# The second mixer's input units in another order, seven of them split into halves instead of fp32

## Chip, cores and metric

The kernel runs on one core of one Trainium2 chip. The metric is device time in microseconds, the median of several runs. Lower is better.

## What is computed

The reference runs two transformer blocks one after the other on x of 256 tokens by 2048 features, in float32. The part that changes is the start of the second block:

```
h = rms_norm(x, mix_norm_g)
proj = h @ w_in                      # 2048 x 4656
q, kv, gate_logits, conv_in = split(proj)
attn = nsa_attention(q, kv, sigmoid(gate_logits), rel_bias, cmp_pos, cmp_w1, cmp_w2)
conv = conformer_conv(conv_in, ...)  # a * sigmoid(gate), causal conv of 31 taps, layer norm, silu
x = x + concatenate([attn, conv]) @ w_out
```

`kv` holds keys and values for three branches: one is compressed by a small MLP over blocks of 32 tokens (`compress`), two are used as they are (the branches 0 and 1 below). `conv_in` is 1024 channels of `a` and 1024 of gate.

## The kernel before

The whole network is one list of units, made by `all_units` (line 138). A unit is 256 output columns of one weight matrix. Its weights come in subs of 512 KB: 4 k-tiles of 128 rows for 256 columns, so an input unit with 16 k-tiles has 4 subs. Activations lie feature-major, 128 features by 256 tokens per tile.

A unit has a mode. In mode `full` the weights go to TensorE as fp32 straight from the landing buffer RAW, against H in fp32. H must first be multiplied in place by the norm weights (`full_u2`, line 1202, on ScalarE, four phases of four tiles). In mode `one` each sub is split: ScalarE writes a rounded high half WH, VectorE writes WL = RAW - WH (`split`, lines 1169 and 1695), and TensorE multiplies three times with 256 columns: high with high, high with low, low with high. Modes `nat`, `turn` and `joint` are forms of the split one. There are 4 RAW buffers and 5 of each half.

The second mixer's input units are, with the names used in this text: a0 to a3 (`ev_ca`, the channels a), g0 to g3 (`ev_cg`, the gate), m0 and m1 (`ev_cmp`, keys and values to compress), k0 and k1 (`ev_k2`), v0 and v1 (`ev_v2`), q0 to q3 (`ev_q2`, queries of four heads each). Before, they run in this order, `full` except a0, g0, v0, v1: a0 g0 m0 m1 a1 g1 k0 k1 a2 g2 v0 v1 q0 a3 g3 q1 q2 q3. Then come the eight units of w_out on the convolution's rows (`ev_add`) and the eight on the attention's.

`make_plan` (line 265) turns the units into one order of steps that every engine follows, each taking those it has a part in. Each engine works its own list strictly in order. After each sub the plan takes one phase from a lane `conv` and one from a lane `side`. When a unit's last sub is in the plan, its evacuation (`evac`) follows (for a0 and pg7 two subs later), and the work it makes possible is appended to a lane: `conv31` of 11 phases (62 instructions of VectorE, 60 of them multiply-adds of 256 columns, six in each phase but the first), `compress` of 3, `dup_k2` of 2, `attn2` of 9, `ln` of 7, `scc` of 1. `before=("side",)` empties the side lane ahead of a unit, `2` makes it two stages wide. `split` of a sub stands 4 subs ahead of it when the sub four places before it in its buffer is split too, else 2 (`lead`, line 294). The fetch of a sub is on SP's queue and waits until its RAW buffer is free: for a split sub after `split`, for a fp32 one after its products. SP's queue also carries the loads of W1K and W1V (`load_w1`, line 656, 1 MB each, weights of `compress`) and of BM (`load_bias`, line 659, 2 MB, the attention's bias). Sub numbers here: a0 562 to 565, g0 566 to 569, then four per unit (v1 six, 606 to 611), q0 612, q3 632 to 635.

A unit's columns go to the next PSUM bank of 0, 1, 2, from q0 on of 0, 1, and TensorE waits until the unit that had the bank is evacuated (`bank_free`, line 766). BLK, GTM and GCM are buffers of `compress`, KTC holds m's or k's columns, TA and TC the gate's and a's, SCC (in SQA) the convolution's sums for the layer norm, SX2, PT2 and RC the attention's, CC the convolution's outputs.

Of the kernel before, what the change touches and what calls it, by code (L numbers as in the profile page):

```python
# [27 lines left out]
HOLD = 2  # L28
LATE = 3
FULL_XBC = 7  # L30

MATS = ["rot", "rdup0", "rdup1", "triu", "negT", "dup0", "dup1", "ident", "ones"]

VECS = [("g_mix", 16), ("cw", 96), ("cb", 24), ("g_ssd", 16), ("dsk", 16), ("g_ffn", 16), ("g_ple", 16),
# [72 lines left out]
def stage(name, i, n, late=0, gaps=()):  # L107

    out = [None] * late
    for ph in range(n):  # L110
        out.append(ph)
        if ph in gaps:
            out.append(None)
    return (name, i, out)
# [15 lines left out]
def attn1_stage(t, late):  # L130
    return stage("attn1", t, 4, late, (1, 2))


def attn2_stage(t, late):
    return stage("attn2", t, 9, late)


def all_units():
    us = []
    add = lambda *p, **k: us.append(Unit(*p, **k))  # L140
    order = lambda i: "turn" if i else "joint"
    wide = (0, 1, 2, 3)
    for i in range(4):
        add("w_in", 0, 16, 256 * i, "U1", "ev_q", i, mode=order(i), mid=(("norm", 0, 0),) if i == 0 else (), hold=2 if i == 0 else 0,
            gens=([stage("rotary", 0, 3)] if i == 0 else []) + [stage("rope_q", i, 2)])
    add("w_in", 0, 16, 1024, "U1", "ev_k", 0, mode="turn", gens2=[stage("full_u1", 0, 4)], gens=[stage("rope_k", 0, 2), stage("rope_k", 1, 2)])
    add("w_in", 0, 16, 1280, "U1", "ev_v", 0, nc=288, more=6656, nat=True, mode="nat",
        gens=[2] + [attn1_stage(t, LATE if t == 1 else 0) for t in range(8)] + [1, stage("cums", 0, 2)])
    for i in range(12):
        add("w_in", 0, 16, 3584 + 256 * i, "U1", "ev_xbc", i, mode="full" if i < FULL_XBC else "turn",  # L150
            gens2=[stage("conv4", i, 3)] + ([stage("dt", 0, 2)] if i == 0 else []))
    for i in range(8):
        add("w_in", 0, 16, 6688 + 256 * i, "U1", "ev_ga", i, mode="turn", before=("all",) if i == 0 else (),
            gens=[stage("ssd", g, 6) for g in range(4)] if i == 0 else (), pace=2)
        add("w_attn_br", 0, 8, 256 * i, "AT", "ev_oa", i, mode="turn", pace=2)
    for i in range(8):
        add("w_in", 0, 16, 1536 + 256 * i, "U1", "ev_z", i, mode="turn", banks=wide,
            before=("side",) if i == 0 else ())
    for i in range(8):
        add("w_in", 0, 16, 8736 + 256 * i, "U1", "ev_gs", i, mode="turn", banks=wide, mid=(("norm", 1, 0),) if i == 0 else (),  # L160
            hold=HOLD if i == 0 else 0)
    for i in range(8):
        add("w_ssd_br", 0, 16, 256 * i, "YH", "ev_os", i, mode=order(i), banks=wide)
    for i in range(8):
        add("w_o", 0, 16, 256 * i, "MH", "ev_h", i, mode=order(i), banks=wide)
    for half in range(2):
        for i in range(11):
            first = half == 0 and i == 0
            add("w_gate", 0, 16, 256 * (11 * half + i), "F1", "ev_g1", 11 * half + i, banks=wide, mode=order(11 * half + i),
                mid=(("norm", 2, 0),) if first else (), hold=HOLD if first else 0)  # L170
            add("w_up", 0, 16, 256 * (11 * half + i), "F1", "ev_u1", 11 * half + i, banks=wide, mode="turn")
        for i in range(8):
            if half and i == 3:
                us[-2].mid = (("load_p", 0, 0),)
                for j in range(8):
                    add("w_ple_proj", 0, 2, 256 * j, "PH", "ev_pp", j, banks=wide)
            add("w_down", 2816 * half, 22, 256 * i, "G1", "ev_h", 8 + 8 * half + i, banks=wide, k0=22 * half,
                mode=order(i))
    for i in range(8):
        add("w_ple_gate", 0, 16, 256 * i, "P1H", "ev_pg", i, mode=order(i), mid=(("norm", 3, 0),) if i == 0 else (),  # L180
            hold=HOLD if i == 0 else 0, banks=wide)

    def ca_cg(i, mode="full", mid=(), **k):
        add("w_in_2", 0, 16, 2608 + 256 * i, "U2", "ev_ca", i, mode=mode, mid=mid[:1] if i else mid, **k)
        add("w_in_2", 0, 16, 3632 + 256 * i, "U2", "ev_cg", i, mode=mode, banks=k.get("banks", (0, 1, 2)),
            mid=(("load_w1", 0, 0),) if i == 0 else (), gens=[stage("full_u2", 0, 4)] if i == 0 else [],
            gens2=[stage("conv31", i, 11)] + ([stage("ln", 0, 7)] if i == 3 else []))

    def k2(br):
        add("w_in_2", 0, 16, 1536 + 512 * br, "U2", "ev_k2", br, mode="full", before=("side",),  # L190
            gens=[stage("dup_k2", br, 2)])

    def q2(i, **k):
        add("w_in_2", 0, 16, 256 * i, "U2", "ev_q2", i, mode="full", gens2=[stage("scc", 0, 1), stage("scc", 1, 1)] if i == 0 else [],
            gens=[attn2_stage(2 * i, 0), attn2_stage(2 * i + 1, 2 if i == 0 else 0)], banks=(0, 1), **k)

    ca_cg(0, "one", (("load_pos", 0, 0), ("join", 0, 0)), hold=HOLD)
    add("w_in_2", 0, 16, 1024, "U2", "ev_cmp", 0, mode="full", mid=(("load_w1", 1, 0),),
        gens=[stage("compress", 0, 3, 1)])
    add("w_in_2", 0, 16, 1280, "U2", "ev_cmp", 1, mode="full", mid=(("load_bias", 0, 0),),  # L200
        gens=[stage("compress", 1, 3, 1)])
    ca_cg(1)
    k2(0)
    k2(1)
    ca_cg(2)
    add("w_in_2", 0, 16, 1792, "U2", "ev_v2", 0, nat=True)
    add("w_in_2", 0, 16, 1792 + 512, "U2", "ev_v2", 1, nc=304, nat=True, mode="nat")
    q2(0, before=("side", 2))
    ca_cg(3, banks=(0, 1))
    q2(1)  # L210
    q2(2)
    q2(3)
    for i in range(8):
        add("w_out_2", 1024, 8, 256 * i, "MXC", "ev_add", i, banks=(0, 1), before=("conv",) if i == 0 else ())
    for i in range(8):
        add("w_out_2", 0, 8, 256 * i, "MXA", "ev_h", 24 + i, mode="turn", banks=wide, before=("side",) if i == 0 else ())
    for half in range(2):
        for i in range(11):
            first = half == 0 and i == 0
            add("w_up_2", 0, 16, FFN + 256 * (11 * half + i), "F2", "ev_g2", 11 * half + i, banks=wide, mode=order(11 * half + i),  # L220
                mid=(("norm", 5, 0),) if first else (), hold=HOLD if first else 0)
            add("w_up_2", 0, 16, 256 * (11 * half + i), "F2", "ev_u2", 11 * half + i, banks=wide, mode="turn")
        for i in range(8):
            add("w_down_2", 2816 * half, 22, 256 * i, "G2", "ev_h" if not half else "ev_fin",
                32 + i if not half else i, banks=wide, k0=22 * half, mode=order(i))
    return us
# [116 lines left out]
def hybrid_block_kernel(nc, a, out):  # L343
# [104 lines left out]
    def mat(n):  # L448
        i = MATS.index(n)
        return M7[:, i, :] if i < 7 else M2[:, i - 7, :]  # L450
# [141 lines left out]
    jn_pe, jn_d, jn_a = steps("join_pe"), steps("join_d", "rr", "ms", "eps", "rec", "ru"), steps("join_root")  # L592
# [1090 lines left out]
    def vector_program(e):  # L1683
# [453 lines left out]
        def ev_cmp(n, u):  # L2137
            kv = u.i
            if kv:
                e.wait_ge(cmp_d.sem, cmp_d.at(0, "b11"))  # L2140
            else:
                e.wait_ge(blank.sem, 2)
            e.wait_ge(sub_done.sem, u.end)
            tt(KTC[:, :, :], bank(u.bank), two(RU[:, 0:T]), MUL).then_inc(cmp_d.sem)
            if kv:
                e.wait_ge(cp_pe.sem, cp_pe.at(0, "w1"))
            else:
                e.wait_ge(pos_k_in, 16)
                e.wait_ge(pos_v_in, 16)
            e.wait_ge(cmp_d.sem, cmp_d.at(kv, "k"))  # L2150
            for lh in range(2):
                for hp in range(2):
                    rows = slice(64 * hp, 64 * hp + 64)
                    o = BLK[lh][rows, :, 30 * hp:30 * hp + 30].rearrange("p l (t n) -> p l t n", t=2)
                    x = bass.AP(KTC, 64 * hp * KTC_T + 16 * lh, [[KTC_T, 64], [1, 16], [T, 2], [16, 15]])
                    y = PSC[rows, kv, 16 * lh:16 * lh + 16].unsqueeze(2).unsqueeze(3).broadcast_to([64, 16, 2, 15])
                    tt(o, x, y, ADD).then_inc(cmp_d.sem)
# [257 lines left out]
        def ev_fin(n, u):  # L2415
# [12 lines left out]
                             ev_cg=ev_cg, ev_cmp=ev_cmp, ev_k2=ev_k2, ev_q2=ev_q2, ev_v2=ev_v2, ev_add=ev_add,  # L2428
# [136 lines left out]
```

## Time and profile before

| | |
|---|---|
| median of 3 runs | 2923.86 us (2923.34 to 2925.53) |
| the profiled execution | 2923.59 us, span 2921.8 us |
| TensorE (PE) busy | 96% of the span |
| VectorE (DVE) busy | 66% |
| ScalarE (ACT) busy | 46% |
| mean granted TensorE clock | 0.983 of full speed |
| moved by DMA | 503 MB, 172 GB/s |

The page names engines PE (matmul), PEld (weight load, beside PE), DVE, ACT, POOL and SP. Matmuls are pipelined, so the records of two neighbours overlap, and the distance between two starts is the price of one. Most instructions are made in helpers and show the helper's line (L747 a matmul, L1685 tensor_tensor, L1693 scalar_tensor_tensor, L1157 activation), so they are told apart by the names of their tiles: PS<-H,raw is an fp32 unit, PS<-BIGt,wh and PS<-wh,BIGt a split one of this mixer.

### The profile page before, as it was taken

Reading aid. Unit: us, or ns where it says so; the run is one execution under the profiler, and the core shown is the slowest. Engines: PE = TensorE matmul, PEld = TensorE weight load, DVE = VectorE, ACT = ScalarE, POOL = GpSimd, SP = SyncE. Lnnn points to the kernel's source line nnn. Section 1 sums busy time; section 2 is a strip of 40 time slices with the busy share of each in tenths; the row PEclk is TensorE's granted clock in tenths of the full one; section 3 lists DMA queues with packets and bytes.
Section 4 is the critical chain, followed back from the end, with each engine's and each line's share of the span. In section 5 each row is a group of like instructions: output and inputs, shape, how many; then the busy total and the mean of one; then the engine's idle time right before and its main releaser. Section 6 shows DMA issues by size and latency. Waiting matters only on the chain.

```text
span 2921.8 us, 40859 instructions
## 1 busy us (share of the span) xinstructions
PE 2808.5 (96%) x16434; PEld 2446.2 (84%) x16434; DVE 1922.3 (66%) x2796; ACT 1342.5 (46%) x2014; POOL 40.4 (1%) x76
## 2 busy tenths in 40 slices
PE   7998898999999999999999989996899999999997
PEld 6887787888888888888888788984888888888886
DVE  7447766856766665566666755657678875577765
ACT  5334454554454443444454530135555554455542
POOL 0310000000000000000000000000000000000000
PEclk9999999999999999999999999997999999999999
DMA  6445443555555656665556444532355556555554
GB/s 219 151 137 190 151 147 116 183 192 188 187 180 195 194 177 197 183 198 186 191 188 197 161 145 158 161 114 92 110 172 187 188 187 196 181 200 177 198 186 132
DMA packets 148092, 503.45 MB, mean 172 GB/s; under 512 B 17280, under 2 KB 24560, under 8 KB 147648
## 3 DMA queue, kind: packets, MB, share of 16 engines
q1 hardware_dynamic: 140944, 488.30, 51.2%
q0 software_dynamic: 3312, 5.89, 0.7%
q10 hardware_dynamic: 3648, 6.66, 0.6%
q8 instruction: 130, 2.13, 0.3%
q14 instruction: 58, 0.48, 0.1%
HBM read 496.55 MB, written 7.41 MB: 172 GB/s over the span
## 4 chain that ended last, share of the span: by engine, by line
PE 89%; DVE 7%; ACT 2%; issue 1%; DMA 0%; ACTq 0%; SPq 0%; DVEq 0%
PE PS L747 88%; DVE wl L1685 2%; ACT wh L1157 1%; DVE SQA L1685 0%; DVE TA L1693 0%; DVE H L1693 0%; DVE TC L1693 0%; DVE TA L1685 0%; ACT TB L1157 0%; DVE Z L1685 0%; DMA raw<-in_w_in 0%; ACT SX2b L1157 0%; DVE AHt L1693 0%; DVE RB L1736 0%; PE PS L1082 0%
## 5 line engine op out<-in xcount | busy, mean ns | idle before, releaser
L1685 DVE TENSOR_TENSOR wl<-raw,wh 128x1024 fp32r<-128x1024 f32 (+2 forms) x856 | 994.8, 1194 | 477.2 <-ACT wh L1157 476.1
L1157 ACT ACTIVATE wh<-raw 128x1024 fp32r<-128x1024 f32 (+2 forms) x856 | 853.3, 1029 | 515.7 <-PE PS L747 438.0
L747 PE MATMUL PS<-CHt,wh 128*128 128x512 f32 x2816 | 885.9, 395 | 1.5 <-DVE wl L1685 1.5
L747 PE MATMUL PS<-AHt,wh 128*128 128x512 f32 (+1 forms) x1984 | 606.8, 386 | 31.4 <-DVE wl L1685 22.8
L747 PEld LDWEIGHTS PS<-CHt,wl 128*128 128x128 f32 x2816 | 529.0, 188 | 124.8
L747 PE MATMUL PS<-BIGt,wh 128*128 128x512 f32 (+1 forms) x1920 | 593.9, 391 | 12.8 <-DVE TA L1685 12.8
L747 PE MATMUL PS<-CHt,wl 128*128 128x256 f32 x2816 | 553.5, 278 | 0.0
L747 PEld LDWEIGHTS PS<-CHt,wh 128*128 128x128 f32 x2816 | 429.3, 189 | 1.9 <-issue 1.7
L747 PEld LDWEIGHTS PS<-BIGt,wl 128*128 128x128 f32 x1856 | 351.3, 189 | 79.2
L747 PEld LDWEIGHTS PS<-AHt,wl 128*128 128x128 f32 x1856 | 353.0, 190 | 75.8
L747 PE MATMUL PS<-AHt,wl 128*128 128x256 f32 x1856 | 379.7, 280 | 0.0
L747 PE MATMUL PS<-BIGt,wl 128*128 128x256 f32 x1856 | 373.2, 279 | 0.0
L747 PEld LDWEIGHTS PS<-AHt,wh 128*128 128x128 f32 x1984 | 310.1, 191 | 38.8 <-DVE wl L1685 14.9
L747 PEld LDWEIGHTS PS<-BIGt,wh 128*128 128x128 f32 x1920 | 297.4, 191 | 14.6 <-DVE TA L1685 13.5
L747 PE MATMUL PS<-H,raw 128*128 128x256 f32 x1344 | 304.2, 385 | 3.1 <-ACT H L1157 3.1
L747 PEld LDWEIGHTS PS<-H,raw 128*128 128x128 f32 x1344 | 254.2, 192 | 43.7 <-issue 9.2
L1157 ACT ACTIVATE Z<-PS 128x512 f32<-128x512 f32 (+1 forms) x80 | 47.1, 590 | 109.5 <-PE PS L747 109.5
L1693 DVE SCALAR_TENSOR_TENSOR CC<-Z,CV,CC 128x256 f32<-128x256 f32 x240 | 96.9, 481 | 0.1
L1685 DVE TENSOR_TENSOR Z<-PS,Z 128x512 f32<-128x512 f32 (+1 forms) x80 | 54.6, 684 | 49.7 <-ACT Z L1157 47.5
L1685 DVE TENSOR_TENSOR H<-H,PS 128x512 f32<-128x512 f32 x104 | 71.2, 685 | 17.7 <-PE PS L747 15.8
L1693 DVE SCALAR_TENSOR_TENSOR TA<-Z,CV,TA 128x256 f32<-128x256 f32 x160 | 69.0, 481 | 15.0 <-ACT TA L1157 14.8
L1157 ACT ACTIVATE BIGt<-TC 128x256 fp32r<-128x256 f32 x88 | 32.0, 410 | 98.5 <-DVE TC L1685 98.5
(286 smaller groups left out, 1650.3 us busy)
## 6 DMA issues: line engine op xcount, KB each, us to landing
raw<-in_w_up SPq DMA_DIRECT2D x264, 512.0 KB, 4.4
raw<-in_w_in SPq DMA_DIRECT2D x232, 512.0 KB, 3.7
raw<-in_w_down SPq DMA_DIRECT2D x132, 512.0 KB, 4.2
raw<-in_w_gate SPq DMA_DIRECT2D x88, 512.0 KB, 4.5
raw<-in_w_down SPq DMA_DIRECT2D x56, 384.0 KB, 3.4
raw<-in_w_ssd_br SPq DMA_DIRECT2D x32, 512.0 KB, 4.3
raw<-in_w_o SPq DMA_DIRECT2D x32, 512.0 KB, 4.2
raw<-in_w_ple_gate SPq DMA_DIRECT2D x32, 512.0 KB, 4.4
```

The lines of the kernel that those rows point to most:

```text
L747: return e.matmul(o, l, r, start=start, stop=stop, skip_group_check=True)
L1157: return e.activation(o, x, f, **k)
L1685: return e.tensor_tensor(o, x, y, op)
L1693: return e.scalar_tensor_tensor(out=o, in0=x, scalar=s, in1=y, op0=o0, op1=o1)
```

## The change

The units come from a string. A letter is the kind, the digit the number, `f` is mode `full`, `S`, `C` and `2` are the entries of `before`, and x and y are the two halves of w_out. The new order is a0 g0 m0 a1 m1 g1 a2 k0 k1 g2 v0 v1 q0 a3 g3 q1 q2 q3. Now `full` are a1, m1, k1, a3, g3, q2, q3. Split are a0, g0, v0, v1 as before, and m0, g1, a2, k0, g2, q0, q1, which were fp32. The three loads W1K, W1V and BM all stand behind g0, where they stood behind g0, m0 and m1. The two `scc` stages of convolutions 0 and 1 follow convolution 2 in the conv lane instead of being appended behind q0. The evacuation of m0 has one more wait, on the joined norm that a0's evacuation already waited for.

```diff
+MIXER = 'a0 g0 m0 a1f m1f g1 a2 k0S k1fS g2 v0 v1 q0S2 a3f g3f q1 q2f q3f xC yS'.split()
...
-    ca_cg(0, "one", (("load_pos", 0, 0), ("join", 0, 0)), hold=HOLD)
-    add("w_in_2", 0, 16, 1024, "U2", "ev_cmp", 0, mode="full", mid=(("load_w1", 1, 0),),
-        gens=[stage("compress", 0, 3, 1)])
-    add("w_in_2", 0, 16, 1280, "U2", "ev_cmp", 1, mode="full", mid=(("load_bias", 0, 0),),
-        gens=[stage("compress", 1, 3, 1)])
-    ca_cg(1)
-    k2(0)
-    k2(1)
-    ca_cg(2)
...
-    q2(0, before=("side", 2))
-    ca_cg(3, banks=(0, 1))
-    q2(1)
-    q2(2)
-    q2(3)
...
+    for what in MIXER:
+        name, i = what[0], int(what[1]) if what[1:2].isdigit() else 0
+        opts = what[1:]
+        k = dict(banks=(0, 1, 2) if three else (0, 1), before=())
...
+        k["mode"] = "full" if "f" in opts else "one"
+        mid = ()
+        if first:
+            mid, k["hold"] = (("load_pos", 0, 0), ("join", 0, 0)), HOLD
+        elif second:
+            mid = (("load_w1", 0, 0), ("load_w1", 1, 0), ("load_bias", 0, 0))
...
+        if name == "a":
+            add("w_in_2", 0, 16, 2608 + 256 * i, "U2", "ev_ca", i, gens=fu, **k)
+        elif name == "g":
+            add("w_in_2", 0, 16, 3632 + 256 * i, "U2", "ev_cg", i, gens=fu, gens2=[stage("conv31", i, 11)] + ([stage("scc", 0, 1), stage("scc", 1, 1)] if i == 2 else []) + ([stage("ln", 0, 7)] if i == 3 else []), **k)
+        elif name == "m":
+            add("w_in_2", 0, 16, 1024 + 256 * i, "U2", "ev_cmp", i, gens=fu + [stage("compress", i, 3, 1)], **k)
...
@@ -2139,6 +2158,7 @@
             else:
+                e.wait_ge(jn_d.sem, jn_d.at(0, "ru"))
                 e.wait_ge(blank.sem, 2)
```

## Rows read from the trace of the kernel before

**Rows 1.** The page: engines, chain that ended last, costliest groups.

```profile
PE 2808.5 (96%) x16434; PEld 2446.2 (84%) x16434; DVE 1922.3 (66%) x2796; ACT 1342.5 (46%) x2014; POOL 40.4 (1%) x76
...
PE 89%; DVE 7%; ACT 2%; issue 1%; DMA 0%; ACTq 0%; SPq 0%; DVEq 0%
...
L1157 ACT ACTIVATE wh<-raw 128x1024 fp32r<-128x1024 f32 (+2 forms) x856 | 853.3, 1029 | 515.7 <-PE PS L747 438.0
...
L747 PE MATMUL PS<-H,raw 128*128 128x256 f32 x1344 | 304.2, 385 | 3.1 <-ACT H L1157 3.1
```

**Rows 2.** Windows: stretch, length, PE, PEld, DVE, ACT, POOL busy, PEclk, DMA share, GB/s.

```profile
1696.50:1725.70 29.20, 29.20 (x216) 28.99 (x216) 14.99 (x19) 10.59 (x15) 0.00 (x0) 0.90 0.37 124
...
1729.05:1755.15 26.10, 26.10 (x113) 22.38 (x114) 14.96 (x32) 4.64 (x12) 0.00 (x0) 0.93 0.51 171
...
1770.49:1782.80 12.31, 12.31 (x53) 10.25 (x50) 7.01 (x20) 0.00 (x0) 0.00 (x0) 0.86 0.46 143
1861.30:1886.30 25.00, 25.00 (x194) 24.97 (x193) 23.53 (x48) 8.66 (x11) 0.00 (x0) 1.00 0.64 205
...
1996.20:2043.60 47.40, 19.96 (x122) 14.55 (x121) 35.88 (x108) 25.01 (x68) 0.00 (x0) 0.64 0.23 88
1696.50:1996.20 299.70, 291.94 (x1724) 256.45 (x1724) 179.65 (x442) 67.84 (x166) 0.00 (x0) 0.98 0.43 139
```

**Rows 3.** Timeline of TensorE: start, length, line, tiles, count, idle before.

```profile
1729.05 26.10 PE L747 MATMUL PS<-H,raw 128*128 128x256 f32 x112 [3.13 <-ACT H L1157]
1755.08 2.08 PE L747 MATMUL PS<-BLK,W1K 128*64 128x60 f32 x32
...
1770.24 0.33 PE L747 MATMUL PS<-GCM,W2C 64*64 64x60 f32 x4 [3.78 <-DVE GCM L1689]
...
1861.79 0.40 PE L747 MATMUL PS<-wh,BIGt 128*128 128x256 f32 x2
...
1872.58 0.40 PE L747 MATMUL PS<-wh,BIGt 128*128 128x256 f32 x2
...
1872.94 0.44 PE L747 MATMUL PS<-wh,BIGt 128*128 128x304 f32 x2
...
1886.34 13.97 PE L747 MATMUL PS<-H,raw 128*128 128x256 f32 x64
```

**Rows 4.** Timeline of VectorE.

```profile
1745.72 3.99 DVE L1685 TENSOR_TENSOR BLK<-KTC,PSC 64x480 f32<-64x480 f32 x4
...
1769.22 0.20 DVE L2167 COPY GTM<-PS 64x60 f32<-64x60 f32 x1
...
1869.58 2.46 DVE L1693 SCALAR_TENSOR_TENSOR CC<-Z,CV,CC 128x256 f32<-128x256 f32 x6
...
1872.97 2.46 DVE L1693 SCALAR_TENSOR_TENSOR CC<-Z,CV,CC 128x256 f32<-128x256 f32 x6
...
1938.29 0.69 DVE L1685 TENSOR_TENSOR TA<-PS,RB 128x512 f32<-128x512 f32 x1 [1.76 <-PE PS L747]
...
1940.40 0.43 DVE L1689 TENSOR_SCALAR Z<-TC 128x512 f32<-128x512 f32 x1
...
1957.52 4.83 DVE L1693 SCALAR_TENSOR_TENSOR CC<-Z,CV,CC 128x256 f32<-128x256 f32 x12
...
1991.89 1.22 DVE L1685 TENSOR_TENSOR wl<-raw,wh 128x1024 fp32r<-128x1024 f32 x1 [4.01 <-ACT wh L1157]
```

**Rows 5.** Timeline of ScalarE.

```profile
1727.21 6.48 ACT L1157 ACTIVATE H<-H,G 128x256 f32<-128x256 f32 x16
...
1939.55 0.79 ACT L1157 ACTIVATE PT2a<-PS 128x768 f32<-128x768 f32 x1
```

**Rows 6.** DMA issues of 1690 to 2050: count, size, median us to landing.

```profile
raw<-in_w_in SPq DMA_DIRECT2D x64, 512.0 KB, 3.6
...
BM<-bias_by_query SPq DMA_DIRECT2D x1, 2048.0 KB, 10.0
...
W1K<-in_cmp_w SPq DMA_DIRECT2D x1, 1024.0 KB, 5.8
```

More of the change, by code:

```diff
@@ L181, in all_units @@
             hold=HOLD if i == 0 else 0, banks=wide)
[L183 to L195, printed above, removed]
-    ca_cg(0, "one", (("load_pos", 0, 0), ("join", 0, 0)), hold=HOLD)
-    add("w_in_2", 0, 16, 1024, "U2", "ev_cmp", 0, mode="full", mid=(("load_w1", 1, 0),),
-        gens=[stage("compress", 0, 3, 1)])
@@ L200, in all_units @@
-    add("w_in_2", 0, 16, 1280, "U2", "ev_cmp", 1, mode="full", mid=(("load_bias", 0, 0),),
-        gens=[stage("compress", 1, 3, 1)])
-    ca_cg(1)
-    k2(0)
-    k2(1)
-    ca_cg(2)
-    add("w_in_2", 0, 16, 1792, "U2", "ev_v2", 0, nat=True)
-    add("w_in_2", 0, 16, 1792 + 512, "U2", "ev_v2", 1, nc=304, nat=True, mode="nat")
-    q2(0, before=("side", 2))
-    ca_cg(3, banks=(0, 1))
-    q2(1)
-    q2(2)
-    q2(3)
-    for i in range(8):
-        add("w_out_2", 1024, 8, 256 * i, "MXC", "ev_add", i, banks=(0, 1), before=("conv",) if i == 0 else ())
@@ L215, in all_units @@
-    for i in range(8):
-        add("w_out_2", 0, 8, 256 * i, "MXA", "ev_h", 24 + i, mode="turn", banks=wide, before=("side",) if i == 0 else ())
+    first = True
+    three = True
+    for what in MIXER:
+        name, i = what[0], int(what[1]) if what[1:2].isdigit() else 0
+        opts = what[1:]
+        k = dict(banks=(0, 1, 2) if three else (0, 1), before=())
+        if "S" in opts:
+            k["before"] += ("side",)
+        if "C" in opts:
+            k["before"] += ("conv",)
+        if "2" in opts:
+            k["before"] += (2,)
+        k["mode"] = "full" if "f" in opts else "one"
[4 more added lines that the diff above has]
+            mid = (("load_w1", 0, 0), ("load_w1", 1, 0), ("load_bias", 0, 0))
+        k["mid"] = mid
+        if first is False and second:
+            fu = [stage("full_u2", 0, 4)]
+        else:
+            fu = []
+        second, first = first, False
+        if name == "a":
[4 more added lines that the diff above has]
+            add("w_in_2", 0, 16, 1024 + 256 * i, "U2", "ev_cmp", i, gens=fu + [stage("compress", i, 3, 1)], **k)
+        elif name == "k":
+            add("w_in_2", 0, 16, 1536 + 512 * i, "U2", "ev_k2", i, gens=fu + [stage("dup_k2", i, 2)], **k)
+        elif name == "v":
+            if i == 0:
+                add("w_in_2", 0, 16, 1792, "U2", "ev_v2", 0, nat=True, **{**k, "mode": "one"})
+            else:
+                add("w_in_2", 0, 16, 1792 + 512, "U2", "ev_v2", 1, nc=304, nat=True, **{**k, "mode": "nat"})
+        elif name == "q":
+            if i == 0:
+                three = False
+                k["banks"] = (0, 1)
+            add("w_in_2", 0, 16, 256 * i, "U2", "ev_q2", i,                 gens=[attn2_stage(2 * i, 0), attn2_stage(2 * i + 1, 2 if i == 0 else 0)], **k)
+        elif name == "x":
+            for i in range(8):
+                add("w_out_2", 1024, 8, 256 * i, "MXC", "ev_add", i, banks=(0, 1), before=k["before"] if i == 0 else ())
+        elif name == "y":
+            for i in range(8):
+                add("w_out_2", 0, 8, 256 * i, "MXA", "ev_h", 24 + i, mode="turn", banks=wide, before=k["before"] if i == 0 else ())
```

## The prediction

> **What bounds the kernel now.** I read the page first: TensorE is busy 96% of the span and the chain that ended last runs 89% over its matmuls, VectorE 7% [rows 1]. So TensorE's time counts nearly everywhere, and VectorE's only where it makes TensorE wait. Then the windows of the second mixer's input units, a0 to q3, which take 1696.5 to 1996.2 [rows 2]: TensorE is busy 291.9 of 299.7 us, VectorE 179.7, ScalarE 67.8, and the DMAs carry 139 GB/s. After it stands a tail to 2043.6 in which TensorE is busy 20 of 47.4 us at a granted clock of 0.64 and VectorE 35.9: the layer norm of the convolution and the attention's chains bind there. The timeline of TensorE names the two stalls in the input part [rows 3]: 3.13 us ahead of m0, released by ScalarE's scaling of H (`full_u2`), and 3.78 us ahead of compress 0's second product, released by VectorE's GCM. After each the clock was down: 0.93 over the 26.1 us behind the first, 0.86 over the 12.3 us behind the second [rows 2].
>
> **Price of a unit.** An fp32 unit is 16 k-tiles x 2 halves = 32 products of 256 columns, and the trace records each in two passes, 64 records. q0's 64 records take 13.97 us at full clock, and one alone 0.385 us [rows 1, 3]; they start (13.97 - 0.385)/63 = 0.216 us apart. A unit costs 64 x 0.216 = 13.80 us, a sub a quarter of it, 3.45. A split unit is 96 products; v0 shows it: 30 groups of three start from 1861.79 to 1872.58, 0.360 us each [rows 3], so 32 x 0.360 = 11.51 us. Changing one from fp32 to halves gives TensorE 2.29 us back. Seven (m0, g1, a2, k0, g2, q0, q1): 16.0 us.
>
> The Trainium skill ("TensorE: Matmul & The Clock Gate", section "Back-to-back issue gap") gives N/2.4 + 2.5 ns for one matmul, 109 ns at 256 columns; 96 of them would be 10.5 us and the seven units would give 23 us. The rows have 120 ns, and they decide.
>
> **The stall ahead of m0.** In the old order m0 is the first fp32 unit and needs H scaled, which ScalarE does in 6.48 us from 1727.21, behind the gate's tanh [rows 5]. In the new one m0 is split and a1 is the first fp32 unit, 11.5 us later. By then (1725.9 + 11.5 = 1737.4) ScalarE is done (1727.2, about 2 us later for m0's splits, + 6.5 = 1735.7). The 3.13 us go, and with them the slow clock: the 112 records behind the stall take 26.10 us, (26.10 - 0.385)/111 = 0.232 each, 112 x (0.232 - 0.216) = 1.8 us. Together 4.9 us. m0's own four splits are due at subs 566 to 569; VectorE has them done by about 1728, TensorE wants the first at 1725.9 and the last at 1734.5. The gate's evacuation comes 2 us later for them; nothing waits for it but the convolution.
>
> **The stall at compress 0.** It stands in the plan behind the first sub of the unit after next. Before, VectorE had m1's 4 us of BLK additions (as the 3.99 us of m0's [rows 4]) ahead of the GTM copy at 1769.22. In the new order a1 sits between m0 and m1, so ahead of GTM stand only a1's evacuation (0.7) and a convolution phase (2.4). Counted from the end of a1: GTM at 3.3, GCM ready at 4.3 (1769.22 to 1770.24 before [rows 3, 4]); TensorE has the W1 product (2.0 [rows 3]) and a sub (3.45) to do, 5.5 us. The wait goes, with 1.2 us in hand: 3.78 us, and the clock behind it, (12.31 - 0.385)/47 = 0.254 against 0.216, x 48 = 1.8. Together 5.6. compress 1 now comes behind g1's first sub: BLK done 5.1 us behind m1's end, TensorE there after two split subs, 5.8 us. It just fits.
>
> **What is added beside TensorE.** 28 splits: ScalarE 28 x 1.03 [rows 1] = 29 us on 68 of 300, VectorE 28 x 1.22 (as the one at 1991.89 [rows 4]) = 34 on 180 of 300. On average there is room; the close place is v0 to q0, since the planner puts splits 4 subs ahead behind split units and 2 ahead behind fp32 ones. VectorE runs split and convolution phase alternately at 1872.97 - 1869.58 = 3.39 us with a 912-wide split [rows 4], 3.5 with a 1024-wide one, against a split sub of 2.9. From the end of g2 (T): evacuation to T + 2.6 (g3's takes from 1938.29 to 1940.83 [rows 4]), v1's splits and phases 0 to 5 to T + 20.7, q0's four splits ready at T + 21.9, 25.4, 28.9 and 32.4. TensorE ends v0 at 11.5 and v1 (1886.34 - 1872.94 = 13.4 [rows 3]) at 24.9, and wants them at 24.9, 27.8, 30.7 and 33.5. No stall, but the last margin is 1.1 us. The rest of convolution 2, then q0's evacuation end near T + 40, when TensorE ends a3's first sub (24.9 + 11.5 + 3.5 = 39.9) and turns to the first attention step: about nothing lost. Lower bound of this cost 0; upper, if a phase and split take 3.9 us instead of 3.5 (the 0.4 us that VectorE sometimes waits between them), 4 us at q0 and perhaps 2 for the clock.
>
> Near k0 convolution 1 fills VectorE: with split 3.5, four times, then phases alone, it ends phase 6 as k0 ends. The dup products behind k0 wait for k0's evacuation as they did. For q1: its second split's high half stands in ScalarE's queue in front of the tanh of g3 and of attention 0's PT2a, which ran at 1939.55 [rows 5] just in time for TensorE; VectorE would take the low half to 1940.7 and only then g3's TA, which ran at 1938.29 [rows 4]. The tanh and then PT2a slip 2.4 to 3.3 us, and TensorE, 0.6 us earlier than before, waits about 0.9. So q1 gives 1.4, not 2.3.
>
> **The moved loads.** W1K, W1V and BM (4.2 MB) now all stand in SP's queue behind the fetch of sub 577, issued when split 573 is done, near 1728. They landed in 5.8, 5.8 and 10.0 us [rows 6], 21.6 one behind the other: done by 1750 at worst. The next fetch, of 578, is issued when sub 574 ends (1741), would land at 1754 behind them, and TensorE wants it at 1755.2 (573 ends 1737.4, four fp32 subs 13.8, two W1 products 4.0). So 0 is taken; upper bound, at the part's mean 139 GB/s [rows 2], 4.2 MB last 30 us and the fetch comes 6 us late, with the clock 8. The Trainium skill ("DMA: Bandwidth & Descriptors", section "Issuing engines are not separate DMA queues") says that all DMAs run on the same 16 engines and interleave: by that the loads would also slow the four fetches in flight. Those are wanted from 1737 on, so it changes nothing in the sum, and no row here shows it.
>
> **The tail.** From q0 on the plan is the same, sub by sub. The tail starts with q3's end: VectorE idled 4.01 us before 1991.89 waiting for w_out's split [rows 4], so convolution 3 was not the last. It works without a pause from 1957.52 [rows 4], and in the new order it comes to that point 1.6 us earlier, TensorE 1.4 to 1.7. The tail keeps its 47.4 us. The two scc steps of convolutions 0 and 1 move from behind q0 to in front of its evacuation, in the T + 40 above.
>
> **Sum.** 16.0 + 4.9 + 5.6 - 0.9 (q1) - 0.2 (the longer first product at each new change from fp32 to halves, two of them) = 25.4 us. The profiled execution took 2923.59 us around its span of 2921.8; 2923.6 - 25.4 = 2898.2. The median of the three runs is 0.3 above that execution, so 2898.5.
>
> **The rivals.**
> - VectorE binds at v0 to q0. For: 23.5 of 25 us busy in v0 and v1 already [rows 2], margins of 1 to 3 us. Against: the sum above closes. Price 4 + 2: 2904.
> - The 4.2 MB hold up sub 578, or the compress wait (1.2 and 0.7 us in hand) stays. 8 us, or 5.6: 2904 to 2907. Against: the stretch 1861.3 to 1886.3 carried 205 GB/s [rows 2], by which the loads take 20 us.
> - Slower than before: the stream binds. The part carries 299.7 x 139 = 41.7 MB. If the DMAs gave it no more than the 124 GB/s of a0 and g0 [rows 2], where units were split too, it would last 336 us, 37 more: 2961. It decides below 139 GB/s, where gain turns to loss. For: split subs want 524 KB per 2.88 us, 182 GB/s. Against: those 205 GB/s, in split units, with no wait of TensorE.
> - Nothing comes of it: VectorE late by as much as TensorE is early, and the tail grows. Convolution 3 would have to be 25 us later against q3; VectorE's 180 + 34 of 274 us speak against. 2923.
> - More comes: the tail's first wait (VectorE 4 us ahead) shortens too, or a clock dip I did not price goes: 2893.
>
> **Chances.** Forecast 0.62, VectorE 0.17, loads or compress 0.11, stream 0.04, nothing 0.03, more 0.03. A change under 0.2% (5.8 us) can't be told from none here. Faster 0.94, same 0.02 (the "nothing" case, less a part that goes to slower), slower 0.04. The range 2894 to 2907 holds the first three cases and half of "more".
>
> **What would show it.** In the new profile: 672 more split products (448 PS<-BIGt,wh, 224 PS<-BIGt,wl) and 896 records PS<-H,raw instead of 1344; the gap before the first fp32 matmul and before GCM's product gone and the clock at 1.00 there; q3's last sub 25 us earlier against 1696.5 and the tail still 47 us. A gap of TensorE released by VectorE's wl within q0, or by a DMA at m1, would show the second and third case. I am wrong if the input part ends less than 18 us or more than 30 us earlier.

## The result, and the profile after

| | before | changed |
|---|---|---|
| median | 2923.90 us (2923.34 to 2925.53) | 2897.16 us (2896.74 to 2899.77) |
| profiled execution, span | 2923.59, 2921.8 us | 2897.46, 2895.6 us |
| ratio, 95% interval | | 0.9909 [0.9896, 0.9921] |

26.7 us less, 0.9%. The forecast was 2898.5, the range 2894 to 2907. A second series of the changed kernel, beside other experiments, gave 2898.29 against 2924.66.

The page of the changed kernel answers to [rows 1]. The fp32 records fell from 1344 to 896, and their idle time of 3.1 us is gone. The instructions of VectorE rose by the 28 splits.

```profile
PE 2790.6 (96%) x16658; PEld 2442.3 (84%) x16658; DVE 1954.9 (68%) x2824; ACT 1372.9 (47%) x2042; POOL 40.6 (1%) x76
...
PE 90%; DVE 6%; ACT 2%; issue 1%; DMA 0%; ACTq 0%; SPq 0%; DVEq 0%
...
L766 PE MATMUL PS<-H,raw 128*128 128x256 f32 x896 | 202.4, 382 | 0.0
```

The windows of the changed kernel, with the columns of [rows 2]: m0 with the first fp32 subs, the stretch around GCM's product, g2 to v1 with VectorE's busiest part, the tail, and the input part as a whole.

```profile
1728.00:1755.00 27.00, 27.00 (x205) 24.72 (x203) 22.87 (x50) 7.04 (x17) 0.00 (x0) 1.00 0.77 257
1758.50:1770.80 12.30, 12.30 (x66) 10.76 (x65) 9.43 (x21) 3.18 (x3) 0.00 (x0) 1.00 0.46 130
1830.00:1871.40 41.40, 41.40 (x330) 41.35 (x329) 38.57 (x71) 16.37 (x20) 0.00 (x0) 1.00 0.60 191
1969.70:2018.40 48.70, 21.43 (x122) 15.88 (x120) 35.86 (x108) 25.12 (x68) 0.00 (x0) 0.61 0.22 86
1696.17:1969.70 273.53, 272.16 (x1948) 250.43 (x1948) 211.85 (x470) 96.58 (x194) 0.00 (x0) 0.99 0.48 152
```

The input part shrank from 299.7 to 273.5 us and TensorE is busy in 272.2 of them. The clock is 1.00 in the two stretches where it was 0.93 and 0.86. The DMAs carry 257 GB/s in the stretch with the three bunched loads. TensorE's timeline, as in [rows 3], shows the fp32 subs following without a gap:

```profile
1736.97 10.53 PE L766 MATMUL PS<-H,raw 128*128 128x256 f32 x48
1747.43 2.08 PE L766 MATMUL PS<-BLK,W1K 128*64 128x60 f32 x32
...
1758.74 0.33 PE L766 MATMUL PS<-GCM,W2C 64*64 64x60 f32 x4
...
1810.14 1.99 PE L766 MATMUL PS<-KTC,M 128*128 128x256 f32 x8 [0.85 <-DVE KTC L1704]
...
1917.94 1.14 PE L766 MATMUL PS<-PT2a,VN 128*64 128x128 f32 x12 [0.51 <-ACT PT2a L1176]
...
1976.45 1.22 PE L766 MATMUL PS<-SQA,M 128*128 128x256 f32 x2 [6.57 <-DVE SQA L1704]
```

48 records take 10.53 us, (10.53 - 0.38)/47 = 0.216 us each: full clock from the first on. Two waits are left in the input part, 0.85 at the dup products as before and the new 0.51 at PT2a. VectorE's timeline, beside [rows 4], shows the place that was worked out as the close one, q0's splits between the phases of convolution 2:

```profile
1856.98 0.47 DVE L1704 TENSOR_TENSOR wl<-raw,wh 128x304 fp32r<-128x304 f32 x1
1857.37 2.46 DVE L1712 SCALAR_TENSOR_TENSOR CC<-Z,CV,CC 128x256 f32<-128x256 f32 x6
1859.74 1.22 DVE L1704 TENSOR_TENSOR wl<-raw,wh 128x1024 fp32r<-128x1024 f32 x1
...
1870.28 1.22 DVE L1704 TENSOR_TENSOR wl<-raw,wh 128x1024 fp32r<-128x1024 f32 x1
1871.41 0.44 DVE L1708 TENSOR_SCALAR GAT<-PS,RB 128x48 f32<-128x48 f32 x2
...
1877.82 0.68 DVE L1712 SCALAR_TENSOR_TENSOR Q<-PS,RB 128x512 f32<-128x512 f32 x1
```

The split and phase pairs run 3.51 us apart ((1870.28 - 1859.74)/3), and q0's evacuation is done at 1878.5, 0.5 us before attention 0's first product at 1878.99, which did not wait.

### The profile page after: what moved, and what is told of

It is laid out like the page before. It is cut to its first block, busy times and chain, and to the rows that moved or that the text cites. A ratio compares the mean times of both kernels' runs of the same rounds, so it can differ in the third digit from the quotient of the medians.

```text
span 2895.6 us, 41391 instructions
## 1 busy us (share of the span) xinstructions
PE 2790.6 (96%) x16658; PEld 2442.3 (84%) x16658; DVE 1954.9 (68%) x2824; ACT 1372.9 (47%) x2042; POOL 40.6 (1%) x76
## 4 chain that ended last, share of the span: by engine, by line
PE 90%; DVE 6%; ACT 2%; issue 1%; DMA 0%; ACTq 0%; SPq 0%; DVEq 0%
PE PS L766 90%; DVE wl L1704 2%; ACT wh L1176 1%; DVE TA L1712 0%; DVE H L1712 0%; DVE TC L1712 0%; DVE TA L1704 0%; ACT TB L1176 0%; DVE Z L1704 0%; ACT SX2b L1176 0%; DVE SQA L1704 0%; DMA raw<-in_w_in 0%; PE PS L1101 0%; DVE RB L1755 0%; ACT DEC L1176 0%
## 5 line engine op out<-in xcount | busy, mean ns | idle before, releaser
L1704 DVE TENSOR_TENSOR wl<-raw,wh 128x1024 fp32r<-128x1024 f32 (+1 forms) x884 | 1028.8, 1195 | 487.1 <-ACT wh L1176 485.9
L1176 ACT ACTIVATE wh<-raw 128x1024 fp32r<-128x1024 f32 (+1 forms) x884 | 883.9, 1031 | 524.7 <-PE PS L766 484.1
L766 PE MATMUL PS<-BIGt,wh 128*128 128x512 f32 (+1 forms) x2368 | 676.2, 371 | 12.8 <-DVE TA L1704 12.8
L766 PEld LDWEIGHTS PS<-BIGt,wl 128*128 128x128 f32 x2080 | 394.2, 190 | 79.2
L766 PE MATMUL PS<-BIGt,wl 128*128 128x256 f32 x2080 | 436.5, 280 | 0.0
L766 PEld LDWEIGHTS PS<-BIGt,wh 128*128 128x128 f32 x2368 | 367.3, 191 | 15.3 <-DVE TA L1704 13.5
L766 PE MATMUL PS<-H,raw 128*128 128x256 f32 x896 | 202.4, 382 | 0.0
L766 PEld LDWEIGHTS PS<-H,raw 128*128 128x128 f32 x896 | 167.3, 190 | 27.4 <-issue 5.5
```

The source lines that it names most:

```text
L766: return e.matmul(o, l, r, start=start, stop=stop, skip_group_check=True)
L1176: return e.activation(o, x, f, **k)
L1704: return e.tensor_tensor(o, x, y, op)
```

## The experiments

All are the changed kernel with another string of units, unless said. So all of them, e1 and e2 too, have the two scc stages behind convolution 2 and, except e4, the bunched loads; the place of the scc stages was not tested by itself. "Beside before" is the median of the run less that of the kernel before on the same chip. The last two columns are read from one profile each and are free of what drifts in the first block. "a0 to w_out" goes from a0's first product to w_out's first, 347.1 us in the kernel before. "Input part" goes from a0's first product to the start of the last transposes (PS<-M,SX2b) ahead of TensorE's wait for the layer norm, 299.07 us before; that is 0.6 us short of the windows above. It leaves out the tail, which takes 48.1 to 49.4 us, mostly by its clock (below). Two profiles of the changed kernel agree in it to 0.03 us, so what a single unit is worth is read from it.

| | what | beside before, us | ratio [95%] | a0 to w_out, us | input part, us |
|---|---|---|---|---|---|
| changed | | -26.7 | 0.9909 [0.9896, 0.9921] | 322.3 | 272.89 |
| changed again | | -26.4 | 0.9911 [0.9897, 0.9924] | 322.2 | 272.92 |
| e1 | new order, nothing more split | -5.4 | 0.9981 [0.9972, 0.9990] | 342.8 | 293.51 |
| e2 | old order, seven split | -20.7 | 0.9929 [0.9916, 0.9941] | 326.7 | 278.45 |
| e3 | m0 in fp32 | -20.4 | 0.9933 [0.9920, 0.9945] | 329.7 | 280.33 |
| e4 | loads at old places | -25.9 | 0.9914 [0.9901, 0.9928] | 323.3 | 274.74 |
| e5 | q1 in fp32 | -24.6 | 0.9915 [0.9902, 0.9929] | 323.1 | 274.56 |
| e6 | all split | +10.3 | 1.0033 [1.0021, 1.0045] | 360.3 | 311.12 |
| e7 | a3, g3 split too | -16.8 | 0.9941 [0.9929, 0.9954] | 330.2 | 281.55 |
| e8 | k1 split too | -23.9 | 0.9919 [0.9906, 0.9933] | 325.9 | 276.69 |
| e9 | m1 split too | -22.6 | 0.9924 [0.9911, 0.9936] | 323.8 | 275.68 |
| e10 | g3 split too | -20.7 | 0.9933 [0.9920, 0.9947] | 329.0 | 279.63 |
| e11 | a3, g3 ahead of v0 | +1.4 | 1.0005 [0.9997, 1.0014] | not comparable | not comparable |

The two ends of the input part, before and changed:

```profile
1995.55 0.82 PE L1082 MATMUL PS<-M,SX2b 128*128 128x128 f32 x6
```

```profile
1969.06 0.82 PE L1101 MATMUL PS<-M,SX2b 128*128 128x128 f32 x6
```

**Changed again**, beside e9 to e11.

> The changed kernel once more, beside the three above, for a comparison on one chip: 26 to 27 us below the kernel before.

Measured -26.4.

**e1, the order alone.**

```diff
-MIXER = 'a0 g0 m0 a1f m1f g1 a2 k0S k1fS g2 v0 v1 q0S2 a3f g3f q1 q2f q3f xC yS'.split()
+MIXER = 'a0 g0 m0f a1f m1f g1f a2f k0fS k1fS g2f v0 v1 q0fS2 a3f g3f q1f q2f q3f xC yS'.split()
```

> The new order and the new place of the loads, but all of m0, g1, a2, k0, g2, q0, q1 in fp32 as before. My theory: only the stall at compress 0 goes (3.8 us) with the slow clock behind it (1.8); the stall ahead of m0 stays at about 3 us, since m0 is still the first fp32 unit. 5.6 us faster than before, near 2918.3. Rival, that the order alone brings nothing and the split units make all the difference: 2923.9. Rival, that the order brings most of it: below 2911.

Measured -5.4, and 5.6 in the input part. In TensorE's timeline of e1 the wait ahead of the first fp32 unit stands, with the slow stretch behind it, and GCM's product follows without a wait:

```profile
1728.72 26.10 PE L766 MATMUL PS<-H,raw 128*128 128x256 f32 x112 [3.13 <-ACT H L1176]
...
1766.06 0.33 PE L766 MATMUL PS<-GCM,W2C 64*64 64x60 f32 x4
```

**e2, the splits alone.**

```diff
+MIXER = 'a0 g0 m0 m1f a1f g1 k0S k1fS a2 g2 v0 v1 q0S2 a3f g3f q1 q2f q3f xC yS'.split()
```

> The old order of units, but the same seven split and the loads bunched behind g0. My theory: 16.0 us from the shorter products, 4.9 from the stall ahead of the first fp32 unit, less about 1 at q1; the stall at compress 0 stays near 3.8 us with its clock, because m1's BLK additions again stand ahead of the GTM copy. 20 us faster than before, near 2904; about 5.6 to 7 slower than the changed kernel. Rival, that the order hardly matters once m0 is split: within 1 us of the changed kernel, 2897. Second question, whether k1 between two split units lets VectorE keep up: a wait of TensorE for WL would show it.

Measured -20.7. The first wait is gone, the second stands to the hundredth as in [rows 3], and TensorE waited for no WL, which answers the second question. So the two parts add: 5.4 + 20.7 = 26.1 against 26.7 by the medians, and 5.6 + 20.6 = 26.2 against 26.2 in the input part.

```profile
1736.82 10.53 PE L766 MATMUL PS<-H,raw 128*128 128x256 f32 x48
...
1762.43 0.33 PE L766 MATMUL PS<-GCM,W2C 64*64 64x60 f32 x4 [3.78 <-DVE GCM L1708]
```

**e3, m0 in fp32.**

```diff
+MIXER = 'a0 g0 m0f a1f m1f g1 a2 k0S k1fS g2 v0 v1 q0S2 a3f g3f q1 q2f q3f xC yS'.split()
```

> The changed kernel with m0 alone back in fp32. My theory: m0 costs 2.3 us more and the wait for the scaled H comes back ahead of it, 3.1 us and 1.8 of slow clock: 7.2 slower than the changed kernel, near 2904.4. Rival, that a unit is only worth its products: 2.3 slower, 2899.5.

6.4 us worse by the medians, 7.4 in the input part. The unit is worth about three times the 2.3 us of its products, because its fp32 form leaves the scaling of H uncovered: the 3.13 us wait and the 112 records in 26.10 us are back, as in e1. From e3's timeline of TensorE:

```profile
1730.40 26.10 PE L766 MATMUL PS<-H,raw 128*128 128x256 f32 x112 [3.13 <-ACT H L1176]
```

**e4, the loads at their old places.**

```diff
-            mid = (("load_w1", 0, 0), ("load_w1", 1, 0), ("load_bias", 0, 0))
+            mid = (("load_w1", 0, 0),)
+        elif name == "m":
+            mid = (("load_w1", 1, 0),) if i == 0 else (("load_bias", 0, 0),)
```

> The changed kernel with the loads back at their old places: W1K behind g0, W1V behind m0, BM behind m1. My theory: the 4.2 MB in one piece cost nothing, so 0 (within 1 us of 2897.2). Rival, that they hold up the fetch of sub 578 or slow the ones in flight: 2 to 6 us faster than the changed kernel.

0.8 us less gain by the medians, within noise, but 1.9 in the input part, of which the tail's clock gave 0.9 back by w_out's first product. The trace shows the cause. BM's 2 MB now go out behind m1 and stand in front of the fetches of split subs. ScalarE waits for the DMA of a sub, VectorE's split of it stands ahead of the GTM copy of compress 1, and TensorE waits there 1.19 us and at the dup products 1.45 instead of 0.85, 1.8 us more in all. First ScalarE's, then TensorE's timeline of e4:

```profile
1783.33 1.06 ACT L1178 ACTIVATE wh<-raw 128x1024 fp32r<-128x1024 f32 x1 [6.21 <-DMA raw<-in_w_in]
```

```profile
1786.58 0.62 PE L768 MATMUL PS<-W2C,GCM 64*15 64x64 f32 x8 [1.19 <-DVE GCM L1710]
...
1811.87 1.99 PE L768 MATMUL PS<-KTC,M 128*128 128x256 f32 x8 [1.45 <-DVE KTC L1706]
```

So the bunched place costs nothing, as forecast, and saves 1.9 us against the old one, which I had not seen. In the changed kernel BM took 15.1 us to land instead of 10.0, and W1V 9.7 instead of 5.8 [rows 6], so they were in by 1744.3.

**e5, q1 in fp32.**

```diff
+MIXER = 'a0 g0 m0 a1f m1f g1 a2 k0S k1fS g2 v0 v1 q0S2 a3f g3f q1f q2f q3f xC yS'.split()
```

> The changed kernel with q1 back in fp32. My theory: q1 is worth 2.3 us of products less the wait of attention 0 for PT2a that its splits on ScalarE cause (0.51 us in the changed kernel's trace): 1.8 slower than the changed kernel. The 0.51 us wait should be gone. Rival, that the splits also delay convolution 3 and so the tail: q1 in fp32 then costs less than 1 us or nothing.

2.1 us worse by the medians, whose interval is 1.3 thousandths or 3.6 us to either side, so they can't separate 1.8 from 1. The input part can: 1.7 worse, as expected, and the 0.51 us wait is gone. The stretch to w_out shows only 0.8, but not for the rival's reason. Had q1's splits held up the tail, its steps would come early in e5; but PT2a's product in the tail stands 316.0 us behind a0's first, against 314.0 in the changed kernel. Only from there to w_out's first product is e5 faster, by its clock (7.1 us against 8.3, the 12 products of PT2a in 1.71 us against 2.03).

**e6, all split.**

```diff
+MIXER = 'a0 g0 m0 a1 m1 g1 a2 k0S k1S g2 v0 v1 q0S2 a3 g3 q1 q2 q3 xC yS'.split()
```

> The new order with every unit split. By TensorE's products alone seven more units give 16 us more. My theory: VectorE, which has 28 more splits of 1.2 us in places that are already full (convolution 1 at k0, convolution 2 at v0 to q0, convolution 3 at q2), makes TensorE wait at the dup products, at q0, at a3 and in front of the layer norm: 0 to 10 us slower than the changed kernel, with waits of TensorE for WL. Rival, TensorE's sum: 16 us faster than it.

37 us worse than the changed kernel, 38.2 in the input part: the direction of my theory, but far outside its 0 to 10. Of the places named, the dup products and q0's evacuation came; the waits for WL that I expected came to 0.47 us in one place. TensorE waits at the small steps of `compress` and of the attention, whose VectorE and ScalarE instructions share their queues with the splits. Four of the waits in TensorE's timeline of e6, at GCM's product, the dup products, q0's evacuation and, inside q3, the SCM products:

```profile
1763.74 0.47 PE L766 MATMUL PS<-GCM,W2C 64*64 64x60 f32 x4 [7.77 <-DVE GCM L1708]
...
1819.56 3.78 PE L766 MATMUL PS<-KTC,M 128*128 128x256 f32 x8 [4.59 <-DVE KTC L1704]
...
1892.88 1.16 PE L766 MATMUL PS<-KD,Q 64*128 64x128 f32 x8 [3.92 <-DVE Q L1712]
...
1989.25 1.01 PE L1150 MATMUL PS<-M,SCMa 128*15 128x128 f32 x4 [4.80 <-DVE SX2a L1704]
```

Over 1696.2 to 1985.0 of e6, TensorE is busy 259.9 of 288.8 us at a clock of 0.94, VectorE 229.9.

**e7, a3 and g3 split too, and e10, g3 alone.**

```diff
+MIXER = 'a0 g0 m0 a1f m1f g1 a2 k0S k1fS g2 v0 v1 q0S2 a3 g3 q1 q2f q3f xC yS'.split()   # e7
+MIXER = 'a0 g0 m0 a1f m1f g1 a2 k0S k1fS g2 v0 v1 q0S2 a3f g3 q1 q2f q3f xC yS'.split()  # e10
```

> The changed kernel with a3 and g3 split as well. Products: 4.6 us less. My theory: a3's four splits stand in VectorE's queue before convolution 2's last phase and q0's evacuation, which comes 4 to 5 us later, so attention 0's first step makes TensorE wait about 4 us, and its clock drops (1.8): 0 to 3 us slower than the changed kernel. Rival, that VectorE has room after q0 (it idled there in the kernel before): 4.6 faster.

Measured 9.9 worse, 8.7 in the input part. The wait at q0's evacuation came out as worked out (3.92), but it was not the whole: four more, 6.35 us together, stand behind it, at the attention's own steps. From e7's timeline of TensorE:

```profile
1884.16 1.23 PE L766 MATMUL PS<-KD,Q 64*128 64x128 f32 x6 [3.92 <-DVE Q L1712]
...
1899.26 0.63 PE L766 MATMUL PS<-KDC,Q 64*128 64x15 f32 x8 [0.67 <-DVE SX2b L1704]
...
1903.72 1.14 PE L766 MATMUL PS<-PT2a,VN 128*64 128x128 f32 x12 [0.78 <-ACT PT2a L1176]
...
1910.98 0.60 PE L1150 MATMUL PS<-M,SCMa 128*15 128x128 f32 x4 [2.20 <-DVE SX2a L1704]
...
1918.49 1.15 PE L766 MATMUL PS<-PT2b,VN 128*64 128x128 f32 x12 [2.70 <-ACT PT2b L1176]
```

e10 was made to tell which of the two matters.

> The changed kernel with g3 split, a3 left in fp32. Products: 2.3 us less. It takes the run with a3 and g3 apart, which lost 10 us instead of my 0 to 3. Theory A, that the loss there came from q0's late evacuation (3.9 us) and what followed from it: g3 alone keeps q0's evacuation in time and is 1 to 2 us faster than the changed kernel. Theory B, that a split unit under the attention's phases is what costs: it is shorter cover for the same chain over ScalarE and VectorE, and its splits stand in that chain; waits at attention 0 and 1's steps of about 6 us in all then remain, and g3 alone is 3 to 6 us slower than the changed kernel.

e10 is 5.7 worse than the changed kernel beside it, 6.7 in the input part, theory B. With q0's evacuation in time the waits of the attention remain, 7.4 us in four places; TensorE's timeline of e10:

```profile
1902.59 0.60 PE L1150 MATMUL PS<-M,SCMa 128*15 128x128 f32 x4 [1.63 <-DVE SX2a L1704]
...
1908.63 0.66 PE L766 MATMUL PS<-PT2a,VC 15*64 15x128 f32 x8 [1.92 <-ACT PT2a L1176]
1912.36 2.03 PE L766 MATMUL PS<-PT2b,VN 128*64 128x128 f32 x12 [3.07 <-ACT PT2b L1176]
...
1924.10 1.15 PE L766 MATMUL PS<-PT2a,VN 128*64 128x128 f32 x12 [0.79 <-ACT PT2a L1176]
```

Theory B gives two reasons: a shorter unit over the attention is shorter cover for the same chain, and its splits stand in the chain. No run tells the share of each.

**e8, k1 split too, and e9, m1 split too.**

```diff
+MIXER = 'a0 g0 m0 a1f m1f g1 a2 k0S k1S g2 v0 v1 q0S2 a3f g3f q1 q2f q3f xC yS'.split()  # e8
+MIXER = 'a0 g0 m0 a1f m1 g1 a2 k0S k1fS g2 v0 v1 q0S2 a3f g3f q1 q2f q3f xC yS'.split()  # e9
```

> The changed kernel with k1 split as well. Products: 2.3 us less. My theory: its four splits stand ahead of k0's evacuation on VectorE, in a stretch that convolution 1 already fills; the dup products wait some 4 us longer than the 0.85 now, with 1.8 of slow clock: 3 to 4 us slower than the changed kernel. Rival: 2.3 faster.

e8: 2.8 worse by the medians, 3.8 in the input part. The wait at the dup products is 4.92 instead of 0.85, 4.1 more as expected, and the products behind it last 3.78 instead of 1.99:

```profile
1814.21 3.78 PE L766 MATMUL PS<-KTC,M 128*128 128x256 f32 x8 [4.92 <-DVE KTC L1704]
```

> The changed kernel with m1 split as well. Products: 2.3 us less. My theory: two of its splits (1.2 us each) stand on VectorE ahead of the GTM copy of compress 0, which had 1.2 us in hand, so TensorE waits about 1 us at GCM's product, too short for the clock to fall: 1 to 1.5 faster than the changed kernel. Rival, that every further split costs more than it gives, as at k1: 2 to 3 slower.

e9: 3.8 worse by the medians (2902.11 against 2898.29 beside it), 2.8 in the input part; my 1 to 1.5 better failed, and the rival's 2 to 3 worse came. GCM's product did not wait. But g1's splits now follow split subs and are planned 4 subs ahead instead of 2, in front of m1's evacuation, so BLK is late for compress 1:

```profile
1776.53 3.67 PE L766 MATMUL PS<-BLK,W1V 128*64 128x60 f32 x32 [4.18 <-DVE BLK L1704]
```

**e11, a3 and g3 ahead of v0 and v1**, an attempt on the tail.

```diff
+MIXER = 'a0 g0 m0 a1f m1f g1 a2 k0S k1fS g2 a3f g3f v0 v1 q0S2 q1 q2f q3f xC yS'.split()
```

> The changed kernel with a3 and g3 ahead of v0 and v1, so that convolution 3 follows convolution 2 at once and the layer norm runs beside q2 and q3, while the attention starts 8 subs later. Theory A: the tail is set by the layer norm; its part (some 20 us before the first attention step) leaves the tail, 10 us or more faster than the changed kernel. Theory B: what leaves the tail comes back behind w_out's first half, where the attention's last pair now has nine phases with nothing beside them: 0 to 10 us slower.

27.8 worse than the changed kernel beside it. w_out's first product comes at 1985.48, 32.4 us earlier than in the changed kernel, each counted from a0: the layer norm does leave the tail, as theory A says. But the attention, 8 subs later, then stands behind w_out's first half with too little beside it. From w_out's first product to the sums of the next norm (PS<-SQA,M) e11 takes 195.7 us, of which TensorE waits 28.5, nearly all of it for the attention's steps, at a mean clock of 0.85; the changed kernel takes 136.1, with 6.7 us of waits and a clock of 0.97. Three windows of e11 in that stretch:

```profile
2000.00:2040.00 40.00, 32.66 (x266) 29.52 (x266) 22.63 (x54) 18.41 (x42) 0.00 (x0) 0.91 0.36 117
2040.00:2080.00 40.00, 33.17 (x252) 30.09 (x254) 22.27 (x53) 21.59 (x52) 0.00 (x0) 0.83 0.28 88
2080.00:2120.00 40.00, 26.27 (x159) 19.24 (x156) 15.72 (x59) 18.79 (x60) 0.00 (x0) 0.59 0.10 30
```

Theory B named the mechanism and undersized it: it put 0 to 10 where 27.8 came.

## Why the prediction was right

- **Price of a unit**, 2.29 us. Right. Up to attention 0's first product (1903.70 before, 1878.99 after, each less its a0 start) the gain is 207.2 - 182.8 = 24.4 us; my terms to there are 6 x 2.29 + 4.9 + 5.6 = 24.2. The Trainium skill ("TensorE: Matmul & The Clock Gate", section "Back-to-back issue gap") gives its N/2.4 + 2.5 ns for an isolated matmul and says that it is too low at small N in a stream of weight loads and matmuls. Taken for the stream all the same, 109 ns at 256 columns, it gave an estimate 7 us higher for the seven units, and the measured 120 ns and this sum don't bear that out.
- **The stall ahead of m0**, 4.9 us. Right: gone with m0 split, there with m0 in fp32 in e1 and e3 (3.13 us, 26.10 us for 112 records). e3 puts the unit with its stall at 7.4 in the input part (6.4 by the medians), against 7.2.
- **The stall at compress 0**, 5.6 us. Right: e1 removes it by the order alone (5.6 in the input part, 5.4 by the medians), e2 keeps it (3.78).
- **VectorE at v0 to q0.** Right within half a microsecond: q0's last split is done at 1871.50, 32.2 us after g2's end (its evacuation starts at 1839.27), where the working had 32.4, and q0's evacuation is done 0.5 us before it is wanted. e7 showed how near that is: a3's four splits in front of it give 3.92 us of wait.
- **q1**, 1.4 us. A little too low: PT2a cost 0.51, not 0.9, and q1 gave 1.8 (26.2 at attention 2's first product less 24.4), or 1.7 by e5.
- **The moved loads**, 0. Right for the place they have; that the old place would now cost 1.9 us in the input part (e4) I had missed.
- **The tail**, "keeps its 47.4 us". Off by 1.3: from the transposes behind q3 to w_out's first product it is 48.1 before and 49.4 after. The steps up to PT2a's product run alike (26.4 us earlier at each from 1976.45 to 2010.13, of which 0.3 stems from a0's earlier start); what differs is the clock behind it. The windows of three steps before w_out, first of the kernel before, then of the changed one:

```profile
2036.00:2039.00 3.00, 2.46 (x18) 2.14 (x20) 0.24 (x1) 1.18 (x2) 0.00 (x0) 0.67 0.00 0
2039.00:2042.00 3.00, 3.00 (x25) 1.84 (x24) 1.94 (x4) 0.17 (x1) 0.00 (x0) 0.76 0.00 0
```

```profile
2009.60:2012.60 3.00, 2.47 (x16) 2.14 (x18) 0.24 (x1) 1.18 (x2) 0.00 (x0) 0.50 0.03 8
2012.60:2015.60 3.00, 3.00 (x20) 2.06 (x17) 1.79 (x4) 0.00 (x0) 0.00 (x0) 0.50 0.00 0
```

The same work had the 1.2 GHz level throughout in the changed kernel and part of it the 2.4 GHz level before. 70 us later the difference is gone: attention 6's transposes start at 2104.96 and 2078.49, 26.5 apart, since there the dip falls the other way (its last value product before them waited 3.99 us and took 1.12 before, 3.37 and 0.66 after). What moves the dip was not tested. The other profiles fall on both sides: up to PT2a's product their tails agree to 0.5 us (40.9 to 41.4), and from there to w_out's first product they take 7.1 to 8.4 us, e5 and e9 as long as the kernel before (7.1), the second profile of the changed kernel as long as the first (8.4 and 8.3).

So the input part gave 26.2 instead of 25.4. The two profiled executions are 26.1 apart, the medians 26.7; what lies between them is inside the spread of the runs. None of the rivals came about here. VectorE late at q0 came in e7, and a wait at compress, at the second one, in e9, as soon as more was split. Of the 12 expectations above, e6, e7, e9 and e11 were wrong. e6 and e7 counted the first places where VectorE or ScalarE would be late and not the ones behind them, e9 looked at compress 0 where compress 1 was late, and e11 had the right mechanism at less than half its size.

## What to carry to other kernels

A change that gives TensorE shorter products is worth their difference only where the other engines' queues have room at that place, not on average: seven units split gave 20.7 us (16.0 of it products by the prediction's sum), and each further one tried alone, k1, m1 or g3, cost 2.8 to 6.7 in the input part. Walk each in-order queue through the new plan, with the splits where the planner puts them, and compare with when TensorE wants the result; margins of 1 us and less held here. The two stalls of 3.13 and 3.78 us on TensorE were each worth about half as much again by the slower clock behind them (1.8 us), so removing a small stall by the order alone (5.6 us for no instruction less) can pay more than a unit's arithmetic (2.3). A stage whose clock varies from one kernel to the next, as this tail does, hides differences of 1 us; measure up to its start.

## What the runs showed of the hardware that was not expected

- The three bunched loads reached 257 GB/s together with the fetches over 1728 to 1755, and each landed later than in the kernel before, where they went out one by one (BM 15.1 against 10.0 us, W1V 9.7 against 5.8), while all three were in by 1744.3, 5.5 us before the 1749.8 that their single times give one behind the other.
- The wait of 3.78 us in e2 and before, and of 3.13 us in e1, e3 and before, repeat to the hundredth, while the same tail, in which TensorE is busy less than half the time, takes 48.1 to 49.4 us from kernel to kernel, mostly by its granted clock.
